# A two-layer hybrid decoder step: new order of the set-up's loads, one weight block across the seam, and VectorE's first expert work re-ordered

## The chip, the core and the metric

One Trainium2 chip, one of its cores. The metric is the device time of one launch, in microseconds (us). Engines: TensorE (PE), VectorE (DVE), ScalarE (ACT), GpSimd (POOL), and SyncE (SP), which issues most of the loads. The median of three runs of the kernel before is 2207.54 us (2205.04 to 2212.47).

## What is computed

One inference step of a decoder of two layers, for 256 prompt tokens and 8 samples of one token each, all in float32, width 1024. Each layer is

```python
def trunk_layer(x, pos, h0, conv_prev, past_lat, past_kr, p):
    h = rmsnorm(x, norm_mix)
    proj = h @ w_in            # gates, z, xBC, dt, c_q, c_kv, k_rope
    ya, h_new, conv_new = ssd_branch(...)          # Mamba-2 scan
    yb, lat_new, kr_new = mla_branch(...)          # latent attention, paged cache for the samples
    x = x + (ga * ya + gb * yb) @ w_out
    x = x + peer(rmsnorm(x, norm_ffn), peer_wq, peer_keys, peer_u, peer_v)
    return x, h_new, conv_new, lat_new, kr_new
```

`peer` is a product-key lookup: per token and head (8 heads) the two halves of a query are scored against 128 keys each, the best 16 of each half are paired, the best 16 pairs give 16 experts; each expert is one row u and one row v of 1024 numbers. Its weight is softmax of the scores times gelu(u . h), and it adds weight times v.

## The kernel before

**Set-up.** A block of its own (L477 to L530) loads the constants, the prompt rows `x`, the row of gains `nrow`, the page table, the samples' rows, and two blocks of the first layer's projection weights into the two slots of `wring`: the first 272 columns of the tail (`TAIL[0]`, with dt) and the first 256 columns of xBC. ScalarE takes the squares of both prompt tiles and a root, VectorE scales them to `h`, TensorE turns them into `ht`. All engines meet at a barrier at its end.

**The layer loop.** `Fori(0, layers)` runs one body twice. Each engine has its own program in the body; they meet in semaphores, and at the end of the body in a barrier (L535 for the end of the block, L2382 for the clearing of semaphores) before the jump back. PSUM banks are handed out by two rings of four: `wide` (banks 0 to 3, emptied by ScalarE) and `aux` (banks 4 to 7, emptied by VectorE). The order on a ring is fixed: VectorE has to empty the `aux` banks in the order in which TensorE fills them.

**Weights.** `next_block` and `load_block` (L542, L2184) use the two slots of `wring` in turn; SyncE waits until a block has been begun (`blocks_begun`) before it loads the next but one. Blocks 0 and 1 of a layer are already there at its start: the set-up has loaded them for layer 0, and the last steps of a layer (L2287 to L2292) load them for the next from `w_first`, an array in which the host lays both side by side. These last steps wait for the last gathered slot and then for both blocks. At a layer's start SyncE issues nine small loads (`vrows`, `hd`, `kvn`, `qn`); TensorE turns `vrows` after the first tail's products, before `dense(0)`, the first use of block 1.

**The expert stage.** 17 units: 8 heads for each of the two prompt tiles (16 slots a unit), and one for the samples (8 slots), 264 slots in all. For each slot GpSimd gathers 128 rows of 8 KB (u and v, 1.05 MB) by the indices of `best_experts` into a ring of 8 places (L2363). VectorE takes the products of rows and tokens (`inputs`, L1770), ScalarE the gelu (L2121), VectorE a scaled diagonal (`diagonal`, L1779), TensorE multiplies it with v and sums in PSUM (`outputs`, L1213), which occupies the `aux` banks; so the first `outputs` waits until `aux` is empty (`marks["x", 1]`). The gather of slot n waits for `outputs(n - 8)`; those of slots 3, 4, 6 and 7 wait in addition for the last readers of the weights that lie in their places: the samples' heads, `out_samples(0)`, `out(2, 1)` and `out(3, 1)`.

`best_experts(u)` is the search of unit u, a generator of 17 steps; VectorE interleaves it with the slots of the unit before, three steps a slot. Into slots 0 to 7 it also puts the late tiles (`late_tiles`): the output projection of tile 1 and of the samples is added to `x` (`out(1, 1)`, two copies of the samples' partial sums to `hp[2]`, `out(2, 1)`, `out(3, 1)`, the samples' additions at L1818), then comes the norm of these tiles (`px_mean`, `px_rows`). TensorE produces them in the same order. ScalarE's squares and root for them stand in its own `late_tiles` (L2133 and L2137).

## Time and profile before

| | us |
|---|---|
| median of three runs | 2207.54 |
| profiled run | 2213.21 |
| its span, first to last instruction | 2211.7 |
| TensorE busy | 1722.7 (78%) |
| VectorE busy | 1443.7 (65%) |
| GpSimd busy | 656.9 (30%) |
| ScalarE busy | 481.4 (22%) |
| DMA | 743.76 MB, 336 GB/s over the span |

Times in the rows are us from the span's start unless marked ns. PE is TensorE's matmuls, PEld its weight loads; a name with a final q (SPq, DVEq) is an engine's queue of instructions, where waits, branches and issues stand. `x2` counts instructions. The bracket at a row's end is the idle time before it and who ended it. PEclk is TensorE's granted clock as a share of 2.4 GHz. The first expert stage lies from 413 to 1102, the second from 1505 to 2195.

### The profile page before, as it was taken

The numbers are of one execution on the slowest core, as the hardware profiler recorded it, in microseconds if no ns is written. First come the engines' busy times: TensorE is split into PE (matmuls) and PEld (weight loads), VectorE is DVE, ScalarE is ACT, GpSimd is POOL, SyncE is SP. The second block draws the span as 40 slices with busy tenths as digits, with TensorE's granted clock in tenths as the row PEclk, the third lists the DMA queues.
The fourth block names the chain that finished last, engine by engine and source line by source line (L and its number), as shares of the span: only waits on it lengthen the run. The fifth ranks groups of instructions, "written<-read, shape, count | busy, mean of one in ns | idle before, by whom it ended". The sixth has DMA issues, their size and how long they took to land. (4 is left out here: it accounts for less than half of the span.)

```text
span 2211.7 us, 30597 instructions
## 1 busy us (share of the span) xinstructions
PE 1722.7 (78%) x11154; PEld 883.6 (40%) x11154; DVE 1443.7 (65%) x3609; ACT 481.4 (22%) x1415; POOL 656.9 (30%) x598
## 2 busy tenths in 40 slices
PE   6999989787787666666779998887878876666665
PEld 5887666532233111111168876664323321111111
DVE  3454443677787887877726554437677788787785
ACT  2235211122112121111213442112211211211112
POOL 0000000145444444454300000003444444444442
PEclk9999999977788676666799999998877886757667
DMA  5448499699999999999854385977999999999997
GB/s 195 145 138 277 140 345 320 247 393 415 419 421 421 420 396 421 421 414 418 360 163 159 117 281 194 363 271 308 390 422 415 410 422 413 416 421 421 417 417 305
DMA packets 190002, 743.76 MB, mean 336 GB/s; under 512 B 16339, under 2 KB 78220, under 8 KB 119682
## 3 DMA queue, kind: packets, MB, share of 16 engines
q0 software_dynamic: 83296, 582.18, 64.3%
q1 hardware_dynamic: 106546, 159.52, 21.1%
q8 instruction: 90, 1.47, 0.3%
q14 instruction: 70, 0.57, 0.1%
HBM read 730.38 MB, written 11.46 MB: 335 GB/s over the span
## 5 line engine op out<-in xcount | busy, mean ns | idle before, releaser
L1213 PE MATMUL ps<-arena 64*64 64x512 f32 x4096 | 755.9, 838 | 395.9 <-DVE arena L1779 375.6
L2363 POOL DMA_INDIRECT arena<-in_peer_uv,arena x528 | 617.9, 1170 | 807.1 <-PE ps L1213 663.6
L1770 DVE CUSTOM_DVE_ANT_0 arena<-arena,h 128x1024 f32<-128x1024 f32 x512 | 627.2, 1225 | 255.8 <-DMA arena<-in_peer_uv,arena 246.7
L1213 PEld LDWEIGHTS ps<-arena 64*64 64x64 f32 x4096 | 141.1, 166 | 953.0 <-DVE arena L1779 876.2
L553 PE MATMUL ps<-ht_tok,wring 128*128 128x264 f32 (+1 forms) x1536 | 368.7, 396 | 7.6 <-DMA wring<-in_w_in 7.6
L553 PEld LDWEIGHTS ps<-ht_tok,wring 128*128 128x128 f32 x1536 | 292.0, 194 | 80.7 <-issue 19.2
L2121 ACT ACTIVATE arena<-arena 128x1 f32<-128x1 f32 x528 | 105.3, 203 | 992.7 <-DVE arena L1770 978.8
L1779 DVE TENSOR_SCALAR arena<-consts,arena 128x64 f32<-128x64 f32 (+1 forms) x528 | 165.0, 313 | 26.7 <-ACT arena L2121 24.2
L553 PE MATMUL ps<-arena,wring 128*128 128x264 f32 x256 | 60.0, 388 | 0.0
L553 PE MATMUL ps<-arena,gate 128*128 128x256 f32 x256 | 58.4, 381 | 0.0
L2342 POOL DMA_DIRECT2D nrow<-in_norm_ffn x2 | 1.1, 533 | 188.6 <-PE ps L562 188.6
L1433 DVE SCALAR_TENSOR_TENSOR h<-h,exs,arena 128x1024 f32<-128x1024 f32 x16 | 20.6, 1284 | 51.0 <-ACT arena L1979 51.0
L2328 POOL DMA_DIRECT2D out<-h x16 | 8.5, 534 | 150.8 <-DVE h L1433 150.8
L553 PE MATMUL ps<-wring,ht_tok 128*128 128x272 f32 (+2 forms) x192 | 44.0, 386 | 11.9 <-ACTq L1870 11.9
L2121 ACT ACT_TABLE_LOAD x40 | 51.3, 1283 | 0.7
L553 PEld LDWEIGHTS ps<-arena,gate 128*128 128x128 f32 x256 | 47.3, 189 | 8.0 <-issue 1.6
L553 PEld LDWEIGHTS ps<-arena,wring 128*128 128x128 f32 x256 | 47.4, 190 | 7.6
L562 PE MATMUL ps<-consts,h 128*128 128x128 f32 (+1 forms) x174 | 36.8, 314 | 14.6 <-ACT h L2044 13.2
L1011 PE MATMUL ps<-arena 128*32 128x256 f32 x512 | 36.1, 401 | 12.4 <-DVEq L1584 12.4
L1701 DVE MAX8 arena<-arena 128x8 f32<-128x128 f32 x136 | 32.9, 283 | 16.9 <-ACT arena L2098 15.8
L2114 ACT ACT_TABLE_LOAD x34 | 43.6, 1283 | 0.8
L1770 DVE DVE_READ_ACCUMULATOR2_ANT arena<- 128x1 f32 x528 | 43.4, 82 | 0.0
(352 smaller groups left out, 1811.7 us busy)
## 6 DMA issues: line engine op xcount, KB each, us to landing
arena<-in_pages SPq DMA_DIRECT2D x256, 272.0 KB, 5.1
wring<-in_w_in SPq DMA_DIRECT2D x36, 1024.0 KB, 5.7
arena<-in_peer_uv,arena POOLq DMA_INDIRECT x528
h<-in_state_ssm POOLq DMA_DIRECT2D x16, 512.0 KB, 5.8
out<-h POOLq DMA_DIRECT2D x16, 512.0 KB, 4.3
wring<-in_w_ssm_proj SPq DMA_DIRECT2D x8, 1024.0 KB, 8.3
arena<-in_w_out SPq DMA_DIRECT2D x8, 1024.0 KB, 8.3
wring<-in_peer_wq SPq DMA_DIRECT2D x8, 1024.0 KB, 7.8
```

Of the source, the lines that this page charges most:

```text
L553: last = pe.matmul(dst, w(c), rhs(c), start=start and c == 0, stop=stop and c == chunks - 1)
L562: return pe.transpose(dst, src, ident[0:rows, 0:rows])
L1011: last = pe.matmul(ps[32 * g:32 * g + 32, b, 0:KV_LORA], pts[:, i % 2, j, g, :], held[:, slot, 2 * g + j, 2 * P + ROPE:KV_ROW], start=j == ...
L1213: last = pe.matmul(ps[to:to + 64, SUM_BANK[t] + i, :], diag[rows, n % DIAGS, 0:64], ring[rows, HOME[n % RING], cols], start=n in TILE_FIRS ...
L1433: dve.scalar_tensor_tensor(out=new, in0=new, scalar=exs[:, SAMPLES + s:SAMPLES + s + 1], in1=stx[:, s % 2, :, :], op0=ALU.mult, op1=ALU.ad ...
L1701: last = dve.max(top[0:r, at[half]], halves[half])
L1770: dve.tensor_tensor_reduce(ring[:, HOME[k], 0:D_MODEL], ring[:, HOME[k], 0:D_MODEL], tokens, 1.0, 0.0, ALU.mult, ALU.add, dots[:, column(n ...
L1779: dve.tensor_scalar(diag[:, n % DIAGS, 0:outs], table[:, 0:outs], gel[:, column(n)], wexp[:, column(n)], ALU.mult, ALU.mult).then_inc(sem( ...
L2114: act.activation(w, w, ACT.Exp, accum_out=wsum[:, u % 2:u % 2 + 1]).then_inc(sem("experts_exp"), 1)
L2121: act.activation(gel[:, at:at + 1], dots[:, at:at + 1], ACT.Gelu).then_inc(sem("gelu_ready"), 1)
L2328: pool.dma_start(h1[b], places[b % PLACES]).then_inc(sem(f"state_store{b % PLACES}"), 16)
L2363: pool.indirect_dma_start(ring[:, HOME[k], :], None, table, bass.IndirectOffsetOnAxis(ap=idx[:, TOPK * u + j:TOPK * u + j + 1], axis=0)).t ...
```

## The change

1. Set-up: the prompt rows load first, then the gain row, the constants, the tail's block, the page table and the samples' rows; every reader waits for what it reads. ScalarE begins with a root of a zero that VectorE writes.
2. Only the tail's block is loaded ahead, in the set-up and at a layer's end; the first xBC block is loaded at the head of the layer by SyncE, before the small loads, and TensorE waits for it at `dense(0)`.
3. The start of the expert stage: ten steps of the search of unit 1 stand before `out(1, 1)` and before slot 0; the two copies follow; slots 0 to 3 have no search steps; the late additions and the norm come one slot or more sooner, and `out(3, 1)` comes after the samples' additions, on TensorE and on VectorE.

```diff
-                sp.dma_start(consts[:, :], a["consts"]).then_inc(sem("first_loads"), 16)
-                sp.dma_start(x[:, 0:2, :], ...).then_inc(sem("first_loads"), 16)
-                sp.dma_start(nrow[:, :], ...).then_inc(sem("first_loads"), 16)
+                sp.dma_start(x[:, 0:2, :], ...).then_inc(sem("x_load"), 16)
+                sp.dma_start(nrow[:, :], ...).then_inc(sem("row_load"), 16)
+                sp.dma_start(consts[:, :], a["consts"]).then_inc(sem("consts_load"), 16)
+                sp.dma_start(wblock(0, DC, TAIL[0][1]), ...).then_inc(sem("first_loads"), 16)
                 sp.dma_start(numbers_held[0:1, :], ...).then_inc(sem("first_loads"), 16)
                 sp.wait_ge(sem("x_zeroed"), 1)
                 sp.dma_start(x[0:SAMPLES, 2, :], ...).then_inc(sem("first_loads"), 16)
-                sp.dma_start(wblock(0, DC, TAIL[0][1]), first[:, :, 0:TAIL[0][1]]).then_inc(sem("first_blocks"), 16)
-                sp.dma_start(wblock(1, DC, BLOCK), first[:, :, TAIL[0][1]:]).then_inc(sem("first_blocks"), 16)
-                sp.wait_ge(sem("first_loads"), 16 * 5)
-                sp.wait_ge(sem("first_blocks"), 32)
+                sp.wait_ge(sem("first_loads"), 16 * 3)
...
             def _(pe):
+                pe.wait_ge(sem("consts_load"), 16)
...
-                act.wait_ge(sem("first_loads"), 16 * 5)
+                act.wait_ge(sem("root_ready"), 1)
+                act.activation(rt[:, 2:3], ss[:, 2:3], ACT.Sqrt)
+                act.wait_ge(sem("x_load"), 16)
...
+                dve.memset(ss[:, 2:3], 0.0).then_inc(sem("root_ready"), 1)
...
-                dve.wait_ge(sem("first_loads"), 16 * 5)
+                dve.wait_ge(sem("row_load"), 16)
...
-                        if n >= 2:
-                            pe.wait_ge(sem(f"block{n % 2}_loads"), 16 * (n // 2))
+                        if n >= 1:
+                            pe.wait_ge(sem(f"block{n % 2}_loads"), 16 * ((n + 1) // 2))
...
                     out(2, 1)
-                    out(3, 1)
                     pe.wait_ge(sem("aux_free"), 4 + marks["sums"])
                     for half in range(2):
                         b = aux.fill()
                         aux.filled(pe.matmul(ps[0:SAMPLES, b, :], cst("sel8"), ...))
+                    out(3, 1)
...
                     ahead = best_experts(1)
+                    for _ in range(10):
+                        next(ahead)
+                    out(1, 1)
+                    for half in range(2):
+                        copy4(hp[2][:, half * 512:(half + 1) * 512])
                     def late_tiles(n):
-                        if n == 0:
-                            out(1, 1)
-                        elif n == 1:
-                            for half in range(2):
-                                copy4(hp[2][:, half * 512:(half + 1) * 512])
+                        if n == 1:
+                            out(2, 1)
                         elif n == 2:
-                            out(2, 1)
-                        elif n == 3:
-                            out(3, 1)
-                        elif n == 4:
                             for half in range(2):
...
+                        elif n == 3:
+                            out(3, 1)
+                        elif n == 5:
+                            px_mean(1, slice(46, 48))
                         elif n == 6:
-                            px_mean(1, slice(46, 48))
-                        elif n == 7:
                             px_rows((1, 2))
...
-                        for _ in range(3 if u != SAMPLE_UNIT else 6):
+                        for _ in range(0 if n < 4 else 3):
...
                     def late_tiles(n):
-                        if n == 5:
+                        if n == 4:
                             act.wait_ge(sem("aux_free"), 4 + marks["x", 1])
-                        elif n == 6:
+                        elif n == 5:
                             root(st[:, 49:51], st[:, 46:48], "px1")
...
-                    count = [2]
+                    count = [1]
                     def load_block(src, chunks, cols):
                         n = count[0]
-                        sp.wait_ge(sem("blocks_begun"), n)
+                        if n >= 2:
+                            sp.wait_ge(sem("blocks_begun"), n)
...
+                    block_of(w_in, XBC, 0)
                     vr = ssd("vrows")
...
-                    sp.dma_start(wblock(0, DC, TAIL[0][1]), first[:, :, 0:TAIL[0][1]]).then_inc(sem("first_blocks"), 16)
-                    sp.dma_start(wblock(1, DC, BLOCK), first[:, :, TAIL[0][1]:]).then_inc(sem("first_blocks"), 16)
-                    sp.wait_ge(sem("first_blocks"), 32)
+                    sp.dma_start(wblock(0, DC, TAIL[0][1]), ...).then_inc(sem("first_block"), 16)
+                    sp.wait_ge(sem("first_block"), 16)
```

The host lays `w_first` out with the tail's columns alone.

## Rows read from the trace of the kernel before

**Rows 1.** The page: DMA busy in 40 slices of 55.3 us.
```profile
DMA  5448499699999999999854385977999999999997
```

**Rows 2.** DMA, GB/s in 40 slices of 1 us from 412 to 452.
```profile
GB/s 0 0 0 205 410 418 279 377 319 385 418 410 442 401 442 426 434 418 434 410 426 410 442 393 90 16 0 0 0 98 147 393 451 401 360 385 451 401 410 426
```

**Rows 3.** Windows: length, PE, PEld, DVE, ACT, POOL busy; PEclk, DMA share, GB/s.
```profile
449.00:462.00 13.00, 13.00 (x56) 4.34 (x48) 7.08 (x14) 4.63 (x10) 6.16 (x5) 0.50 1.01 423
462.00:478.00 16.00, 12.95 (x80) 7.93 (x80) 8.31 (x27) 2.27 (x10) 5.24 (x5) 1.00 1.01 420
490.00:495.00 5.00, 5.00 (x40) 2.05 (x38) 4.67 (x12) 0.92 (x5) 1.93 (x2) 1.00 0.55 215
418.98:448.18 29.20, 18.17 (x108) 9.21 (x105) 27.38 (x74) 6.67 (x16) 11.31 (x10) 0.82 0.81 323
```

**Rows 4.** Timeline of set-up: start, us, engine, instruction, idle before it.
```profile
10.10 1.06 ACT L506 ACTIVATE h<-x 128x1024 f32<-128x1024 f32 x1 [7.82 <-DMA x<-in_x_sample]
...
12.31 1.28 ACT L509 ACT_TABLE_LOAD   x1
...
15.38 3.40 PE L499 MATMUL ps<-consts,h 128*128 128x128 f32 x16 [15.38 <-DVE h L524]
...
20.62 1.28 ACT L1882 ACT_TABLE_LOAD   x1 [6.81 <-PEq L532]
```

**Rows 5.** DMA, GB/s in 40 slices of 0.5 us from 0 to 20.
```profile
GB/s 0 0 0 0 179 298 358 406 302 345 360 401 401 401 377 311 270 287 316 361 355 359 359 357 351 349 350 346 350 346 162 6 0 0 0 0 0 0 0 0
```

**Rows 6.** L477, the first barrier: duration ns, first and last start.
```profile
L477 SPq COMPARE_BRANCH  x1: 33/33/33, 16.2 to 16.2; - x1
...
L477 DVEq COMPARE_BRANCH  x1: 47/47/47, 19.6 to 19.6; - x1
```

**Rows 7.** Issue of L2290's load, then landing of L2290's and L2291's.
```profile
L2290 SPq DMA_DIRECT2D wring<-in_w_first x2: 576/580/583, 1102.2 to 2194.6; - x2
...
DMA to landing us min/median/max: 5.8/5.9/5.9
...
DMA to landing us min/median/max: 8.0/8.1/8.1
```

**Rows 8.** L535, the seam's barrier in both layers: duration ns, starts.
```profile
L535 DVEq COMPARE_BRANCH  x2: 52/52/52, 1107.4 to 2199.8; - x2
...
L535 SPq COMPARE_BRANCH  x2: 33/36/38, 1111.1 to 2203.5; - x2
```

**Rows 9.** Timeline of TensorE at the second layer's start.
```profile
1116.53 6.06 PE L553 MATMUL ps<-wring,ht_tok 128*128 128x272 f32 x16 [10.02 <-ACTq L1870]
...
1129.54 1.15 PE L562 MATMUL ps<-consts,arena 84*128 84x84 f32 x13
```

**Rows 10.** Timeline at the start of the first expert stage.
```profile
403.85 0.49 DVE L1701 MAX8 arena<-arena 128x8 f32<-128x128 f32 x2 [5.40 <-ACT arena L2098]
...
409.51 0.09 DVE L1722 MATCH_VALUE_LOAD arena<-arena 128x8 f32 x1
...
412.72 0.37 ACT L2098 COPY arena<-ps 128x256 f32<-128x256 f32 x1 [3.65 <-PE ps L1097]
...
418.98 1.23 DVE L1770 CUSTOM_DVE_ANT_0 arena<-arena,h 128x1024 f32<-128x1024 f32 x1 [5.22 <-DMA arena<-in_peer_uv,arena]
...
420.01 7.21 PE L553 MATMUL ps<-arena,gate 128*128 128x256 f32 x32
...
427.35 1.88 PE L1159 MATMUL ps<-h,consts 128*8 128x512 f32 x4
...
437.90 8.05 PE L1213 MATMUL ps<-arena 64*64 64x512 f32 x56 [8.67 <-DVE x L1818]
...
440.19 0.97 POOL L2363 DMA_INDIRECT arena<-in_peer_uv,arena  x1 [10.96 <-PE ps L1213]
```

**Rows 11.** Timeline of GpSimd: gather 27 of layer 0, gather 8 of layer 1.
```profile
492.76 1.49 POOL L2363 DMA_INDIRECT arena<-in_peer_uv,arena  x1 [5.46 <-PE ps L1213]
...
1531.83 0.97 POOL L2363 DMA_INDIRECT arena<-in_peer_uv,arena  x1 [10.95 <-PE ps L1213]
```

More of the change, by code:

```diff
@@ L2285, in _ @@
                         count[0] += 1
-                    first = of_layer("next_first", layer).rearrange("(p c) n -> p c n", c=DC)
                     sp.wait_ge(sem("wide_full"), marks["q", 7])
                     sp.wait_ge(sem(f"slot{(SLOTS - 1) % RING}_loads"), 16 * (SLOTS // RING))
-                    sp.dma_start(wblock(0, DC, TAIL[0][1]), first[:, :, 0:TAIL[0][1]]).then_inc(sem("first_blocks"), 16)
-                    sp.dma_start(wblock(1, DC, BLOCK), first[:, :, TAIL[0][1]:]).then_inc(sem("first_blocks"), 16)
-                    sp.wait_ge(sem("first_blocks"), 32)
+                    sp.dma_start(wblock(0, DC, TAIL[0][1]), of_layer("next_first", layer).rearrange("(p c) n -> p c n", c=DC)).then_inc(sem("first_block"), 16)
+                    sp.wait_ge(sem("first_block"), 16)
                 @block.gpsimd
@@ L2433 @@
     laid["peer_uv"] = np.concatenate([np.asarray(inputs["peer_u"]), np.asarray(inputs["peer_v"])], axis=2).reshape(DEPTH * N_EXPERTS, ROW)
-    first = laid["w_in"][:, :, [*range(C_DT, C_DT + TAIL[0][1]), *range(XBC, XBC + BLOCK)]]
+    first = laid["w_in"][:, :, C_DT:C_DT + TAIL[0][1]]
     laid["w_first"] = np.concatenate([first, first[0:1]], axis=0)
```

6 lines of the change are left out of this document (3 added, 3 removed).

## The prediction, written before any run of the changed kernel

> **What bounds the kernel now.** I read the page's DMA slices first. They stand at nine tenths in two long stretches [rows 1]: these are the two expert stages, one a layer, in which GpSimd gathers 264 slots of rows of 1.05 MB each. There no compute engine sets the pace; a slot takes 1.05 MB / 0.42 MB per us = 2.5 us of transfer, and the stage lasts as long as its transfers and the times in which they run dry. So the second view is the slices of one us behind the first gather. They are full from 416, then nearly empty from 436 to 443 [rows 2]: set against 422 GB/s, these eight slices miss 6.2 us of transfer. A smaller drought lies at 490 to 495 (DMA share 0.55) [rows 3]. Outside the expert stages, in the set-up and at the two seams between layers, one chain of engines ends each barrier; there I read who comes last.
>
> **Part 1, the set-up.** ScalarE starts on the rows at 10.10, when all five loads are in, and from there to TensorE's first transpose at 15.38 runs one chain [rows 4]. The slices of 0.5 us give the bytes: they add up to 1.05 MB (the input rows alone) at 5.35 and to 2.34 MB (rows, gain row, constants) at 9.0 [rows 5]. The five loads are 2.37 MB, in by about 9.1, and the wait ended near 10.05: up to 0.9 from last byte to release. With the rows first, ScalarE starts at 5.35 + 0.9 = 6.25. Its chain to the transpose was 15.38 - 10.10 = 5.28 us, a table load of 1.28 in it (12.31); the new Sqrt ahead of the wait takes that load before the rows are there. That the squares then need no table of their own is seen in the loop, where the same order (Sqrt on a constant, squares, Sqrt) has the load at 20.62 and no other [rows 4]. So h is ready at 6.25 + 5.28 - 1.28 = 10.25. The constants are in at 9.0 + 0.9 = 9.9, the gain row before them: hidden by 0.35 us, and one for one beyond that. The first transpose moves by 15.38 - 10.25 = 5.1 us. Last to the barrier is VectorE at 19.6, SyncE comes at 16.2 [rows 6]; VectorE's goes to 14.5. SyncE now waits for 3.49 MB, by the same slices in at 12.4 + 0.9 = 13.3, 1.2 before VectorE. Bounds: 4.0 if the rows' transfer is shared with those behind it, 5.4 if a release takes 0.6. I take 5.1.
>
> Here the Trainium skill and a row differ. The row has the table load of 1.28 us, and the chain of 5.28 has room for no more. The Trainium skill (ScalarE: Activation LUTs, What ACT_TABLE_LOAD costs) counts about 2.66 us for a switch of tables, a drain included. By the page the set-up would give 1.4 us more; the trace does not bear that out here.
>
> **Part 2, the seams.** At a layer's end SyncE issues two blocks, the first at 1102.2; they land after 5.8 to 5.9 and 8.0 to 8.1 us, at 1108.1 and, issued 0.8 later, at 1111.1 [rows 7]. The second does not hold back the first (they land 3.0 us apart, which is 1.05 MB at 350 GB/s), so alone it lands at 1108.1 too. Last to the barrier is SyncE at 1111.1; VectorE comes at 1107.4 [rows 8]. Without the second block SyncE comes at 1108.1 and is still last. Gain 3.0; 3.7 at most, where VectorE is next. The end of the second layer shows the same times 1092.4 later [rows 8], so 6.0 in all.
>
> **Part 3, the block at the head of the layer.** The XBC block's load goes to the front of SyncE's queue, ahead of nine small loads: one more issue (0.5 us) and 1.05 MB before them, 5.9 us to land by the seam's block [rows 7]. TensorE reads the first small ones (the rows for vt) at 1129.54, 13 us after the layer's first product at 1116.53, and waited for none [rows 9]; behind the block they land 6 to 7 us after it. The block itself is needed 1.1 us after them. Cost nothing, under the first tail's products, with 6 us to spare; with that cover gone up to 3 us a layer. The later blocks wait for the same starts as before.
>
> **Part 4, the start of the expert stage.** Why does the transfer run dry? The ring holds eight slots, and slot 8's gather waits for slot 0's output products. TensorE starts these at 437.90, after 8.67 us of waiting for VectorE's sample additions (L1818) [rows 10]. VectorE did the late additions one a slot, between row products and search steps; before that it idled 5.22 us, from 413.76 until slot 0 landed at 418.98 [rows 10].
>
> The new order on VectorE in layer 0: at 413.76 it is through with out(0,1), and ScalarE has put out the scores of unit 1 at 412.72 + 0.37 = 413.1. Ten search steps took 403.85 to 409.51 = 5.66 for unit 0 [rows 10], so to 419.4. The other steps are taken from start to start in the same timeline. out(1,1) is 0.34 and the two copies are 1.2: 421.0. Slot 0 and its weights (1.15 + 0.46): 422.6. Slot 1, diagonal 0, out(2,1) (1.15 + 0.26 + 0.34): 424.35; TensorE has out(2,1) at 420.01 + 3.6 = 423.7. Slot 2 lands at 424.7 (three slots are in at 423.8 [rows 2], + 0.9): 0.35 of waiting; with diagonal 1 and the sample sums (1.2) 427.3. TensorE has the sums' products at 423.7 + 1.88 = 425.6 [rows 10], in time. out(3,1) now follows them and ends at 429.2; VectorE, through with slot 3 and diagonal 2 at 428.7, waits 0.5 and has it at 429.65. TensorE starts slot 0's output products at 429.8 instead of 437.90. From that start to gather 8 were 2.3 us (440.19) and to its first bytes 1.6 (98 GB/s in the slice of 441): 429.8 + 3.9 = 433.7, ahead of the ring's end at 436.3. The first drought goes whole, with 2.6 us in hand. Slot 7's gather, behind out(3,1), is issued at 429.4, with bytes from 431.6 (2 us), and is needed at 433.8: covered by 2 us.
>
> That is not yet the gain. From slot 7 on, products follow VectorE's diagonals, and the second drought (gather 27, issued at 492.76 after 5.46 us of waiting for TensorE [rows 11]) sits at the end of a chain without a transfer: TensorE full from 449 to 462 (13.00 of 13) at clock 0.50 [rows 3], then queries, scores, the search of unit 2. What moves is that chain's start, the end of slot 7's diagonal at 448.18. From 418.98 to there VectorE has 29.20 us, one wait of 1.04 in them (for slot 0's products); the row's busy 27.38 leaves 0.8 of steps between instructions [rows 3]. So 28.16 of work, the same in the new order; begun at 413.76 it ends at 441.9, and with the new waits (0.35, 0.5, and some 0.15 for the late tiles' root) at 442.9. The chain starts 5.3 us earlier, I take 5.2. The transfers would be 6.2 to 6.5 earlier, so the second drought grows by about 1.2, and the stage is 5.2 shorter. Behind it the transfers are full, and all later steps are counted by slot. In layer 1 gather 8 waits 10.95 us for TensorE in the same way [rows 11]: 5.2 again. The last unit's three steps instead of six change nothing, no search is left there.
>
> **The sum.** 5.1 + 6.0 + 0 + 2 x 5.2 = 21.5 us. The span of 2211.7 goes to 2190.2, the profiled run's 2213.21 to 2191.7. The median of the runs is 5.67 below that run: 2207.54 - 21.5 = 2186.0.
>
> **Rivals.** A, the clock stays up. TensorE's stretch from 449 to 462 ran at 1.2 GHz though it was busy throughout [rows 3]. At 2.4 GHz the transfers would set its pace, which are 6.2 to 6.5 ahead, and 3 us of the second drought could go too: 6.5 to 9.5 a layer, 24 to 30 in all, 2183 to 2177. For it: the pause of 8.67 us goes. Against: from 433 to 443 TensorE will have little to do, and the row shows a busy engine held at 0.50. 0.2. The Trainium skill (TensorE: Matmul & The Clock Gate, Part 1) has the gate follow how busy the array was of late, and by it the busy engine of that row should have been fast; the row says otherwise.
> B, the expert stage gives nothing: the second drought takes all back because ScalarE, whose other steps keep their order, holds the queries' place, or the first one stays because the output products still wait. Then 11.1 in all, 2196.4. Against it: TensorE, not ScalarE, is full in that chain. 0.17.
> C, slower. Between 462 and 478 TensorE worked 12.95 us at 2.4 GHz [rows 3]. Should the new phase hold these products and queries at 1.2 GHz, the second drought grows by 13 a layer: 26 - 21.5 = 4.5 slower, 2212. It decides from 10.8 us a layer on. 0.03.
> D, the change does less than it says: the small loads bind, or the rows land no earlier. 2 to 5 us less, 2188 to 2191. 0.05.
> The forecast has 0.55, with a range of its own from 2182 to 2190 (the bounds above and 2 us of scatter).
>
> **Range and chances.** From the far half of A, 2178, to just short of B, 2195: the forecast, D, most of A and a third of B, about 0.8. A measurement of this kernel tells 0.3% (6.6 us) from no change. Below 2200.9 lie the forecast, A, D and nearly all of B: 0.91; within 0.3% 0.06; slower 0.03.
>
> **What would show it.** ScalarE's first square near 6.2 and no table load before its root; the first barrier's last arrival near 14.5; SyncE at the seam's barrier 5.9 us after its one issue; no wait of TensorE over 1 us for L1818; gather 8 about 16.6 us after the first bytes (now 24.7) and no empty slices behind slot 7; gather 27 about 72 us after the first bytes (now 77.3), with a drought some 1.2 us longer than now. The prediction is wrong if gather 8 comes later than 19 us, gather 27 before 70 or after 75, or if TensorE waits for a small load at a layer's head.

## The result, and the profile after

The changed kernel takes 2185.98 us (median of four runs, 2180.19 to 2188.55), the kernel before 2210.01 in the same comparison (2205.04 to 2212.84): a ratio of 0.9889, interval 0.987 to 0.9908, or 24.0 us by the medians. The forecast was 2186.0 and a gain of 21.5 us. The run whose profile follows is the fastest of its four (2180.19 us, span 2178.6). The profiled run of before is slower than its median, so these two traces lie 33.0 us apart, and 9 us of that is not the change. Where this comes from is a large part of what the experiments had to settle.

Set-up, after: ScalarE's first square and the root, TensorE's first transpose, then the last arrivals at the first barrier.

```profile
6.16 1.06 ACT L505 ACTIVATE h<-x 128x1024 f32<-128x1024 f32 x1 [3.66 <-DMA x<-in_x_prompt]
...
8.58 0.20 ACT L508 ACTIVATE st<-st 128x2 f32<-128x2 f32 x1 [0.23 <-DVE st L518]
...
10.45 3.65 PE L496 MATMUL ps<-consts,h 128*128 128x128 f32 x16 [10.45 <-DVE h L524]
```

```profile
L477 SPq COMPARE_BRANCH  x1: 33/33/33, 12.5 to 12.5; - x1
...
L477 DVEq COMPARE_BRANCH  x1: 47/47/47, 14.9 to 14.9; - x1
```

Set against [rows 4, 6]: the first square 3.94 us sooner, no table load in front of the root, the first transpose 4.93 us sooner, VectorE last to the barrier at 14.9 instead of 19.6. The layer's first product starts at 15.96 instead of 20.65: 4.7 us.

The seams, after: the one load's issue and landing, and who comes last to the barrier (both layers).

```profile
L2291 SPq DMA_DIRECT2D wring<-in_w_first x2: 333/333/333, 1081.9 to 2165.4; - x2
...
DMA to landing us min/median/max: 5.0/5.0/5.0
```

```profile
L535 SPq COMPARE_BRANCH  x2: 33/36/38, 1086.9 to 2170.5; - x2
L535 DVEq COMPARE_BRANCH  x2: 52/52/52, 1087.0 to 2170.2; - x2
```

Against [rows 7, 8]: the load alone lands after 5.0 us, not after 5.8 to 5.9, so SyncE comes 3.9 us sooner after its issue. VectorE, which came 3.7 us ahead of it before, is now level with it.

The head of the second layer, after: TensorE's turn for vt, the products on the block that is now loaded at the head (1106.95), and the first products on the block behind it.

```profile
1105.88 1.14 PE L562 MATMUL ps<-consts,arena 84*128 84x84 f32 x13
1106.95 7.39 PE L553 MATMUL ps<-ht_tok,wring 128*128 128x264 f32 x32
1114.72 10.50 PE L553 MATMUL ps<-ht_tok,wring 128*128 128x264 f32 x46 [0.38 <-DMA wring<-in_w_in]
```

No wait for a small load and none for the moved block: the head costs nothing. The 0.38 us at 1114.72 are for the third block, which is loaded as before; TensorE waited 1.35 us for it in the same place of the trace before.

The start of the expert stage in layer 0, after. First the DMA engines' GB/s in 40 slices of 1 us from 400 to 440 (the first gather is issued at 401.0), then TensorE and GpSimd in the timeline.

```profile
GB/s 0 0 98 188 418 385 328 393 295 418 401 401 410 451 442 401 434 410 434 401 434 451 418 401 434 426 442 401 393 467 418 418 401 426 434 434 410 393 434 442
```

```profile
417.65 2.81 PE L1213 MATMUL ps<-arena 64*64 64x512 f32 x24 [0.58 <-DVE x L1660]
...
434.58 1.70 PE L562 MATMUL ps<-consts,h 128*128 128x128 f32 x6
...
442.66 3.83 PE L553 MATMUL ps<-ht_tok,wring 128*128 128x264 f32 x16
```

```profile
419.05 0.94 POOL L2363 DMA_INDIRECT arena<-in_peer_uv,arena  x1 [0.76 <-PE ps L1213]
...
473.01 1.49 POOL L2363 DMA_INDIRECT arena<-in_peer_uv,arena  x1 [5.29 <-PE ps L1213]
```

The eight poor slices of [rows 2] are gone. TensorE starts slot 0's output products 16.6 us after the first gather (before: 24.6) and waits 0.58 us instead of 8.67 [rows 10]; gather 8 follows after 0.76 us. Gather 27 is issued 72.0 us after the first gather (before: 79.5).

### The profile page after: what moved, and what is told of

Read it like the earlier page. It is cut to its first block and busy times, and to the rows that moved or that the text cites. A ratio compares the mean times of both kernels' runs of the same rounds, so it can differ in the third digit from the quotient of the medians.

```text
span 2178.6 us, 30595 instructions
## 1 busy us (share of the span) xinstructions
PE 1705.1 (78%) x11154; PEld 879.4 (40%) x11154; DVE 1443.5 (66%) x3610; ACT 480.5 (22%) x1415; POOL 658.2 (30%) x598
## 5 line engine op out<-in xcount | busy, mean ns | idle before, releaser
L1213 PE MATMUL ps<-arena 64*64 64x512 f32 x4096 | 744.2, 825 | 391.9 <-DVE arena L1779 383.8
L1011 PE MATMUL ps<-arena 128*32 128x256 f32 x512 | 35.2, 394 | 12.3 <-DVEq L1584 12.3
```

The lines of the kernel that those rows point to most:

```text
L1011: last = pe.matmul(ps[32 * g:32 * g + 32, b, 0:KV_LORA], pts[:, i % 2, j, g, :], held[:, slot, 2 * g + j, 2 * P + ROPE:KV_ROW], start=j == ...
L1213: last = pe.matmul(ps[to:to + 64, SUM_BANK[t] + i, :], diag[rows, n % DIAGS, 0:64], ring[rows, HOME[n % RING], cols], start=n in TILE_FIRS ...
```

## The experiments

Times in the tables are medians. The three groups of runs have each their own runs of the kernel before: 2209.3, 2210.45 and 2209.7 us.

### The parts, each by itself, and a second trace of after

**The set-up alone** (both blocks still loaded):

```
-sp.dma_start(consts ...)  -sp.dma_start(x ...)  -sp.dma_start(nrow ...)     # all "first_loads"
+sp.dma_start(x ...)       # x_load
+sp.dma_start(nrow ...)    # row_load
+sp.dma_start(consts ...)  # consts_load
 sp.dma_start(wblock(0, ...), first[:, :, 0:TAIL[0][1]]).then_inc(sem("first_blocks"), 16)
 sp.dma_start(wblock(1, ...), first[:, :, TAIL[0][1]:]).then_inc(sem("first_blocks"), 16)
+act.activation(rt[:, 2:3], ss[:, 2:3], ACT.Sqrt)     # ahead of ScalarE's first wait
```

> The kernel before with the set-up's part alone: the rows load first, each load has its own semaphore, Sqrt on a constant ahead of ScalarE's first wait; both weight blocks are still loaded there and at the seams. By the sum of places read in the two traces (the theory): ScalarE's first square near 6.2 us, TensorE's first transpose near 10.4 (before 15.38). But SyncE then waits for the second block too, 1.05 MB behind the rest: by the slices of the set-up (350 to 400 GB/s) about 3 us after the 13.3 us that I gave SyncE with one block, so the barrier ends near 16 instead of 14.5. 3.2 to 4.7 us faster than before. The rival, that the set-up's gain is given back later in the layer (a wait on the weight blocks takes it), gives 0 to 1 us in total and a shift of the later instructions that shrinks back to zero within the first 100 us.

**One block alone:**

```
-sp.dma_start(wblock(1, DC, BLOCK), first[:, :, TAIL[0][1]:]).then_inc(sem("first_blocks"), 16)   # set-up and seams
+block_of(w_in, XBC, 0)                                                                         # head of the layer
```

> The kernel before with one weight block at the start and across each seam, the next block's load at the head of the layer; nothing else. The traces of before and after give 3.5 and 3.8 us for the two seams, so 7.3 us, and 0 at the heads. The set-up gains nothing, since VectorE and not SyncE ended its barrier: 7.3 us faster, 6.0 by the prediction's term. The rival, that the head gives the seam's gain back (small loads behind 1.05 MB, TensorE waits for the rows of vt or for the block), gives 0 to 3 us in all, and would show as a TensorE wait of 1 us or more within 15 us of the layer's first product.

**The expert stage alone** (the four hunks on TensorE's sums, VectorE's late tiles and search, ScalarE's late tiles):

```
-                    out(3, 1)          # TensorE, ahead of the sample sums' products; now behind them
+                    for _ in range(10):
+                        next(ahead)
+                    out(1, 1)          # and the copies; then out(2,1), sums, out(3,1) with slots 1, 2, 3
```

> The kernel before with the expert stage's part alone (ten search steps ahead, late additions sooner, their root one slot sooner, the sample sums' products ahead of out(3,1)). Theory one (the order and the clock): TensorE starts slot 0's output products some 8 us sooner against the first gather, the chain behind slot 7 starts 3 to 3.6 us sooner, and its transposes and outputs, at 2.4 instead of 1.2 GHz, are 4 us shorter: 7.9 us in layer 0 and 7.9 to 9.8 in layer 1, 16 to 18 in all. Theory two (the prediction's term, the order alone): 5.2 a layer, 10.4 in all, with the stretch of transposes still at 1.2 GHz. Were it under 2 us, the traces' difference in the stage would belong to the two runs and not to the change.

**The changed kernel again:**

> The changed kernel once more, for a second trace. The two traces at hand differ by 33.0 us, the medians by 24.0; 7 us of the 33 arise between 195 and 385 us of layer 0 and 5 us are lost again between 1160 and 1480 in layer 1, where nothing was changed. Theory: these come and go with TensorE's granted clock in single executions (the trace of before has four short falls to 1.2 GHz in layer 0's middle and one in layer 1's, that of after none and four). Then this trace has its falls at other counts, its middle stages differ from the first trace of after by up to 7 us, and set-up (first barrier at 15.9), seams and expert stage repeat within 0.5 us. The rival, that the change itself moves the middle (other loads meet there), gives the same middle in both traces of after.

| run | median us | ratio to before | interval |
|---|---|---|---|
| set-up alone | 2207.16 | 0.9988 | 0.9977 to 0.9999 |
| one block alone | 2199.59 | 0.9964 | 0.9951 to 0.9977 |
| expert stage alone | 2198.21 | 0.9954 | 0.9937 to 0.9972 |
| after again | 2183.87 | 0.9883 | 0.9869 to 0.9898 |

The parts give 2.7, 8.0 and 10.2 us by their ratios, 20.8 together; the whole gives 25.8 here (22.5 to 28.9 by its interval). One block alone is where both traces had put it (7.3 us). The expert stage alone gives 10.2 us (6.2 to 13.9), near the forecast's 10.4 and not the 16 to 18 that I had read from the first pair of traces.

The set-up alone falls short of the 4.7 us that it gives in after (2.7 us, 0.2 to 5.1), and its trace says where. TensorE's first products of the layer, and the first on the third block:

```profile
L477 SPq COMPARE_BRANCH  x1: 33/33/33, 16.3 to 16.3; - x1
```

```profile
31.46 7.39 PE L556 MATMUL ps<-ht_tok,wring 128*128 128x264 f32 x32
40.68 1.60 PE L556 MATMUL ps<-ht_tok,wring 128*128 128x264 f32 x6 [1.83 <-DMA wring<-in_w_in]
```

SyncE, with the second block to wait for, is now last to the barrier at 16.3 (VectorE: 14.7), so the layer starts 3.3 us sooner and not 4.7: that much of the set-up's part needs the one block. TensorE then waits 1.83 us for the third block, where in the trace before it waited 0.31 us (at 41.96), and 1.3 us of the gain are left at that point. This second wait is not shown to be an effect of the set-up: in layer 0 it varies from 0 to 2.1 us over the 14 traces of this study, and it is 1.84 us in the trace of the late additions alone (below), whose set-up is that of before. What the 5 us are by which the parts fall short of the whole stays open in the same measure: 1.4 us are the barrier's, the rest is within the intervals of the four runs.

The second trace of after is the run that changed the reading. I had expected its expert stages to repeat within 0.5 us; they are 3.6 and 5.8 us longer. Each layer's expert stage, from its first to its last gather, in all the traces that matter (worked out from the gathers' issues), with TensorE's stretch behind slot 7 (from the first transpose of the later rows to the first queries, so the same six groups of instructions):

| trace | stage, layer 0 / 1 (us) | stretch (us) | slot 7's diagonal ready, after the first gather |
|---|---|---|---|
| before | 673.4 / 674.0 | 12.3 / 13.1 | +34.9 / +34.7 |
| after, first trace | 665.4 / 663.7 | 8.1 / 8.0 | +31.2 / +30.2 |
| after again | 669.0 / 669.5 | 12.3 / 12.4 | +30.0 / +29.9 |
| expert stage alone | 670.4 / 669.9 | 12.4 / 12.4 | +30.8 / +29.9 |

The same kernel, the same order, and 8.0 or 12.3 us for the same work. Windows of after (first line) and of after again, over that stretch; the columns are those of [rows 3]:

```profile
434.58:442.66 8.08, 8.08 (x52) 3.85 (x49) 4.98 (x11) 2.95 (x7) 3.38 (x4) 0.95 1.01 420
```

```profile
434.00:446.40 12.40, 12.40 (x53) 4.41 (x49) 5.23 (x12) 4.71 (x11) 5.16 (x4) 0.51 1.01 420
```

TensorE is full in both. It runs at 2.4 GHz in one and at 1.2 GHz in the other. The stretch differs by 4.3 us, gather 27 by 3.2 and 5.3 us (+75.2 and +75.3 in after again, +72.0 and +70.0 in after), the stage by 3.6 and 5.8. That the difference goes through to the stage's end can be read from the gathers: from gather 27 to the last one it is 593.1 to 595.1 us in both layers of all twelve traces in which the queries keep their place (594.0 in before, 593.4 in after, 593.8 in after again, layer 0). So the change and the clock act on the stage ahead of gather 27 alone.

The forecast's reading of before's stretch (full, clock 0.50 [rows 3]) and rival A's doubt are both right, one execution each. The Trainium skill (TensorE: Matmul & The Clock Gate, Part 1) has the gate follow how busy the array was of late. By that rule both stretches would be fast: the first trace of after agrees (0.95), the second does not, it is another row in which the array is busy throughout and held at 0.51.

What the second drought did is seen in slices of 5 us, after again first from 470 us, then after from 470, then before from 485; against 422 GB/s they miss 4.9, 2.5 and 3.7 us of transfer:

```profile
470.00:475.00 5.00, 5.00 (x19) 4.04 (x16) 4.86 (x12) 0.20 (x1) 1.02 (x1) 0.65 0.92 324
475.00:480.00 5.00, 5.00 (x39) 2.08 (x38) 4.67 (x10) 0.98 (x5) 2.55 (x2) 1.00 0.46 143
480.00:485.00 5.00, 5.00 (x34) 2.94 (x36) 3.21 (x9) 0.63 (x4) 2.91 (x3) 1.00 0.97 388
```

```profile
470.00:475.00 5.00, 5.00 (x40) 2.22 (x38) 4.85 (x12) 0.84 (x4) 1.69 (x2) 1.00 0.77 320
475.00:480.00 5.00, 5.00 (x32) 3.44 (x32) 3.11 (x9) 0.78 (x4) 3.00 (x3) 1.00 0.96 324
480.00:485.00 5.00, 4.66 (x44) 1.72 (x36) 2.92 (x6) 3.47 (x7) 4.12 (x3) 1.00 1.01 413
```

```profile
485.00:490.00 5.00, 5.00 (x19) 3.27 (x12) 4.86 (x13) 0.20 (x1) 1.02 (x1) 0.56 1.01 421
...
495.00:500.00 5.00, 5.00 (x32) 3.43 (x32) 3.21 (x8) 0.63 (x4) 2.75 (x3) 1.00 0.94 336
500.00:505.00 5.00, 4.57 (x40) 1.78 (x32) 2.71 (x7) 3.75 (x7) 4.27 (x4) 1.00 1.01 405
```

(The slice from 490 to 495 of before stands in [rows 3].) With the stretch at 1.2 GHz the second drought grows by 1.2 us, which is the forecast's figure; at 2.4 GHz it shrinks by 1.2 (layer 0 of one trace each).

**The middle of the layers.** The first pair of traces also drifts apart by 7.6 us in layer 0 between the layer's first product and its first gather, nearly all of it between 195 and 385 us, where nothing was changed, and back by 4.4 us in layer 1. Windows of before and of after, from 26 us to the first gather:

```profile
26.00:413.31 387.31, 364.58 (x2951) 288.04 (x2950) 177.43 (x372) 107.60 (x315) 17.61 (x30) 0.98 0.65 224
```

```profile
26.00:401.04 375.04, 351.76 (x2926) 279.25 (x2926) 177.15 (x371) 107.39 (x314) 15.04 (x27) 1.00 0.67 230
```

The mean clock is 0.98 in one and 1.00 in the other. Over the traces of this study (14 with the two first ones) the time from layer 0's first product to its first gather is 385.2 us + 0.52 us for each us that TensorE spent at 1.2 GHz between 26 us and that gather (correlation 0.92). Counted from the first product itself it is 0.46 (0.88), and in layer 1 0.41 (0.95). Six of the 14:

| trace | us at 1.2 GHz | first product to first gather |
|---|---|---|
| before | 17.1 | 392.7 |
| expert stage alone | 13.7 | 391.4 |
| one block alone | 6.8 | 388.7 |
| after again | 3.4 | 385.8 |
| after | 0.0 | 385.1 |
| search alone (below) | 0.0 | 384.3 |

Kernels with and without the change lie about the same line, most within 1.5 us of it; the farthest off is the trace of the late additions alone, 3.2 us above. So up to 9 us in one trace's middle go with the clock of the execution and not with the kernel; a pair of traces can't be subtracted there. The runs without a trace say the same in the large: of the twelve of the late additions alone, the fastest (2192.71 us) has a mean granted clock of 0.836 and the slowest (2217.43) one of 0.821, with a correlation of -0.93 over the twelve; of the twelve of the expert stage alone it is -0.78.

### Filling TensorE's pauses

If the clock decides about 4.3 us a layer, work for work's sake in the pauses ahead of the stretch should win them. The idle products write a PSUM bank that nothing reads:

```
+def keep_busy(n):
+    for _ in range({0: 28}.get(n, 0)):      # after: {2: 5, 3: 8, 4: 7}, and {16: 10, 17: 7, 18: 3}; second try on before: {0: 14, 7: 4}
+        pe.matmul(ps[:, wide.fill(), 0:256], ident, consts[:, 0:256], start=True, stop=True)
 for n in range(SLOTS):
+    keep_busy(n)
     outputs(n)
```

> The kernel before with 28 products of 128x256 whose result nobody reads, in TensorE's pause of 8.67 us ahead of slot 0's output products; all else as it was. The clock theory: the granted clock no longer falls 18 us behind the first gather, the transposes and outputs behind slot 7 (12.3 us at 1.2 GHz in the trace of before, 8.1 us at 2.4 GHz in the first trace of after) run at 2.4 GHz, gather 27 comes at +75.5 instead of +79.5 us behind the first gather, and a layer's expert stage is 3.5 to 4.5 us shorter though the first drought (gather 8 at +26.9) stays: 7 to 9 us in all, ratio near 0.9965. The rival, that only the order of the work on VectorE sets the second drought: gather 27 stays within 0.7 us of +79.5, the time within 1.5 us of before; if the filling holds real products back, up to 2 us slower a layer.

> The changed kernel with idle products of 128x256 (5, 8 and 7) ahead of the output products of slots 2, 3 and 4, where TensorE waits 1.5, 2.5 and 2.1 us for diagonals. The two traces of after differ in one thing there: in the first the clock is low from 24 to 34 us behind the first gather, in the second from 24 to 45 us, through the transposes; the stage is 665.4 and 663.7 us in the first, 669.0 and 669.5 in the second. The clock theory: with the pauses filled the clock stays at 2.4 GHz, gather 27 comes at +70 to +72 instead of +75.2, and the stage is 664 to 665 us in both layers, every time: 8 to 10 us faster than the typical run of after (2184), near 2175, and with less scatter. The rival (the long stages of the second trace have another cause, or the fall of the clock doesn't hang on these pauses): within 2 us of 2184, or slower by the filling, 1 to 3 us.

> The same with idle products also ahead of slots 16, 17 and 18 (10, 7 and 3), where TensorE waits 3.1, 2.1 and 0.9 us. There both traces of after have 10.2 us of low clock, in which two slots' outputs take 1.98 instead of 1.09 us and the first queries behind them 5.36 instead of 3.83: 3.3 us, ahead of a drought of about 3 us of transfer in which gather 27 waits 5.3 us for TensorE. The clock theory: these 3.3 us come off the drought, gather 27 at +68 to +69, 2.5 to 3 us a layer beyond the variant with the first filling alone, near 2169 to 2170. The rival: the drought is set by VectorE's diagonals of slots 16 to 18, and the second filling brings under 1 us in all.

> The first filling of before was twice too long: 28 products were 56 instructions and took 12.35 us in a pause of 8.67, and ahead of slot 7 a pause of 3.1 us stayed, behind which the clock fell again (38 to 52 us behind the first gather). Here 14 products (28 instructions, 6.2 us) stand ahead of slot 0's outputs and 4 (1.8 us) ahead of slot 7's, where before pauses 2.3 us. The clock theory: no low clock from 35 to 49 us behind the first gather, the stretch from slot 7's transposes to the first queries takes 8.0 instead of 12.3 us, gather 27 comes at +75.3 instead of +79.5, and a stage takes 669.3 instead of 673.7 us: 8.5 us faster in all, ratio near 0.996. The rival (the stretch is long for another reason than its clock, or its length doesn't carry through to the stage): 673 to 674 us a stage and the time within 1.5 us of before.

| run | median us | ratio | interval | stages | stretch |
|---|---|---|---|---|---|
| before, filled with 28 | 2216.22 | 1.0022 | 1.001 to 1.0034 | 675.6 / 676.0 | 12.7 / 11.9 |
| before, filled to size | 2204.9 | 0.9982 | 0.9965 to 0.9998 | 673.0 / 673.0 | 12.7 / 11.4 |
| after, filled ahead of 2 to 4 | 2180.84 | 0.9874 | 0.9857 to 0.9892 | 665.8 / 666.2 | 8.0 / 8.0 |
| after, filled in both places | 2184.31 | 0.9882 | 0.9866 to 0.9897 | 666.0 / 664.8 | 8.8 / 8.0 |

The first filling of before missed its size: one product of 128x256 is two instructions, and

```profile
427.31 12.35 PE L1202 MATMUL ps<-consts 128*128 128x256 f32 x56
```

overfills a pause of 8.67 us, so it showed only that 3.4 us on the output products cost 2 us a stage. The stretch stayed at 1.2 GHz, and the run came out 4.9 us slower by its ratio, where I had expected 7 to 9 us faster.

The filling sized to the pauses is the useful one. In layer 0 it did not hold the clock (10.2 of the stretch's 12.7 us at 1.2 GHz). In layer 1 it kept the clock up until the stretch's last outputs (2.1 of its 11.4 us at 1.2 GHz), and the stretch still took 11.4 us and the stage 673.0, against 674.0. The median is 4.0 us below before (0.4 to 7.7), between the 8.5 us of the clock theory and the 1.5 us of its rival; the two stages of its trace give 1.5 us of that, and where the rest comes from is not shown. TensorE and VectorE in that stretch, and the window around it:

```profile
1533.07 1.09 PE L1218 MATMUL ps<-arena 64*64 64x512 f32 x8 [0.41 <-DVE arena L1785]
...
1540.54 1.98 PE L1218 MATMUL ps<-arena 64*64 64x512 f32 x8 [1.41 <-DVE arena L1785]
```

```profile
1534.05 1.23 DVE L1776 CUSTOM_DVE_ANT_0 arena<-arena,h 128x1024 f32<-128x1024 f32 x1 [1.04 <-DMA arena<-in_peer_uv,arena]
```

```profile
1532.00:1536.00 4.00, 3.59 (x21) 1.94 (x25) 2.48 (x6) 1.07 (x4) 2.40 (x2) 1.00 1.02 426
```

TensorE is at 2.4 GHz in this window and waits for diagonals, VectorE waits 1.0 us for each slot, the transfers are full: behind the first drought the rows themselves are late and set the pace, and the clock's 4.3 us are not there. How much of the drought has to go first is not shown. It need not be all: the late additions alone (below) still miss 4.2 us of transfer there, against 6.2 in before, and their stretch took 7.98 us at 2.4 GHz. In after, where it is closed, the filling ahead of slots 2 to 4 held the clock in both layers, and the stretch took 7.98 us both times. The stages are 3.3 us shorter than in after again, with gather 27 at +70.6 and +71.5. I had expected 664 to 665 us and a time near 2175; the stages are 1 us longer and the median is 2180.84. The interval overlaps that of after (0.9869 to 0.9898), so this is no proven gain over it.

The second filling brought nothing: I had expected 2169 to 2170, and gather 27 at +68 to +69; it came at +71.6 and +70.8. That is what its rival said, though not for the reason that the rival gave. No slice of it is at 1.2 GHz from the first gather to gather 27, and yet:

```profile
454.68 4.58 PE L1202 MATMUL ps<-consts 128*128 128x256 f32 x20
...
464.45 1.56 PE L1202 MATMUL ps<-consts 128*128 128x256 f32 x6
465.94 1.09 PE L1218 MATMUL ps<-arena 64*64 64x512 f32 x8
466.96 3.83 PE L553 MATMUL ps<-ht_tok,arena 128*128 128x264 f32 x16
470.72 3.69 PE L1218 MATMUL ps<-arena 64*64 64x512 f32 x32
```

The idle products ahead of slot 16 (20 instructions, 4.58 us in a pause of 3.05, again about 1.5 times what fits) hold slots 16 to 18 back: against the first filling alone, slot 18's outputs end 1.9 us later behind the first gather, and the queries behind them, at 2.4 GHz, still 1 us later. What a filling of the right size would give there is not shown.

### The place of the queries

> The changed kernel with head 3's three steps on TensorE (queries, queries, scores) three, two and one slots later (behind slots 21, 24 and 27 instead of 18, 22 and 26). In both traces of after gather 27 waits 5.3 us for slot 19's outputs, which stand behind the first of these queries (5.4 us at 1.2 GHz, 3.8 at 2.4), while slot 19's diagonal is ready at about +66. Theory: what is left of the second drought (2.5 us of transfer in after) is this queue place: gather 27 at +68 to +70 in a trace whose stretch ran at 2.4 GHz and +71.5 to +73 where it ran at 1.2, 2 to 2.5 us a layer, 4 to 5 in all, near 0.986. The rival: VectorE's slots 16 to 18 with three search steps each (3 us a slot against 2.5 of transfer) set the drought, or the queries' new place makes another behind slot 21: under 1 us, or slower by up to 3.

> The same with the filling ahead of slots 2, 3 and 4, which kept the clock up in the stretch behind slot 7 (7.98 us in both layers) and gave stages of 665.8 and 666.2 us. If the two add up: gather 27 at +68 to +69, stages of 663.5 us, 8 to 12 us faster than after with its stretch at 1.2 GHz, near 2175, ratio near 0.984. If the queries' place is worth nothing: 0.987 to 0.988, as the filling alone (0.9874).

```
-        at = (2, 6, 10) if hh > 2 else (11, 12, 14)
+        at = (5, 8, 11) if hh == 3 else (2, 6, 10) if hh > 2 else (11, 12, 14)
```

2189.54 us, 0.9894 (0.9871 to 0.9918), and with the filling 2185.82, 0.9875 (0.985 to 0.99). Gather 27 did come sooner, at +66.9 instead of +70.0 in layer 1, where the stretch ran at 2.4 GHz as in the first trace of after; with the filling at +67.6 in both layers. But the stage took 663.9 us (after: 663.7), and in layer 0, at 1.2 GHz, 669.9 (after again: 669.0). GpSimd waits behind slot 21 instead, at gather 30, which needs the place of slot 22:

```profile
1574.59 1.49 POOL L2363 DMA_INDIRECT arena<-in_peer_uv,arena  x1 [4.35 <-PE ps L1213]
```

The drought moves with the queries and is paid either way. The rival holds: with the queries moved, 597.0 to 598.0 us lie between gather 27 and the last gather in the four stages of these two runs, instead of 594, so gather 27 alone no longer tells the stage's length. This trace is also the best picture of the two cases, since both are in one execution: 669.9 us with a stretch of 12.05, 663.9 with one of 7.98.

### The two halves of the expert stage's part

```
 late_only:   out(1, 1) and the copies ahead of the slots, out(2,1), sums, out(3,1) with slots 1, 2, 3; no steps ahead
 search_only: ahead = best_experts(1)
+             for _ in range(10): next(ahead)       # 0 steps with slots 0 to 3; late additions as before
```

> The kernel before with the expert stage's order of late additions alone: out(1,1) and the copies ahead of the slots, out(2,1), the sample sums and out(3,1) with slots 1, 2 and 3, the root a slot sooner; the search keeps three steps a slot from slot 0. Two theories on where the stage's gain comes from. By counting VectorE's work: ahead of slot 0's output products now stand four slots with their 12 search steps instead of five with 15, and 1.5 us of additions and copies have moved into the idle 5.2 us, so these products start 4.5 to 5 us sooner than in before (+24.6), near +20, and gather 8 near +22; the first drought is some 4.5 us shorter. The stage then gains what reaches slot 7's diagonal: about 1.5 us moved into the idle time, 1.5 to 2 us a layer, 3 to 4 in all (0.9985). Were the first drought itself what counts, it would gain 4.5 a layer, 9 in all.

> The kernel before with the ten search steps ahead alone (none with slots 0 to 3, three a slot from then on); the late additions keep their slots, with slots 0 to 4. VectorE's count: 5.7 us of steps fill the idle 5.2 us; ahead of slot 0's output products there are 13 steps instead of 15. They start 5 to 6 us sooner than in before (+24.6), near +19; gather 8 near +20. The stretch behind slot 7 starts 3.5 to 4.5 us sooner (+32.3 to +33; +36.7 in before): nearly all that both parts give together (3.6 to 4.4), since moving late additions from slot to slot takes no work off VectorE. The stage gains that, and 4.3 us more where the clock stays up in the stretch. Rival: the two halves share the gain, the search alone gives 2 us and the early additions the rest (with them alone the stretch started at +35.6, 1 us sooner).

Late additions alone: 2205.18 us, 0.9973 (0.9953 to 0.9992). Search alone: 2204.89, 0.9978 (0.9958 to 0.9998). The intervals leave 1.8 to 10.4 us for the one (6.0 by its ratio, expected 3 to 4) and 0.4 to 9.3 for the other (4.9). The medians can't say whether the halves need each other: 6.0 and 4.9 add up to 10.8, the expert stage alone gives 10.2. The traces, one of each, say that they do. Slot 7's diagonal was ready 1.4 and 2.3 us sooner than in before, with both halves 4.8 in after again (+34.9 to +30.0 in layer 0) and 4.4 in the expert stage alone, all as means of both layers: 0.7 to 1.1 us more than the two together. I had expected 1.5 to 2 for the one, which nearly came, and 3.5 to 4.5 for the other, which did not; slot 0's output products also came later than I had worked out, at +21.4 (expected near +20) and +20.8 (near +19). VectorE's waits from the first gather to slot 7's diagonal tell why: before, search alone, late additions alone, after again.

```profile
DVE arena L1770 <- DMA arena<-in_peer_uv,arena: 5.2, 1, 5.2
DVE arena L1779 <- PE ps L1213: 1.0, 1, 1.0
```

```profile
DVE arena L1770 <- DMA arena<-in_peer_uv,arena: 2.8, 3, 1.5
DVE arena L1779 <- PE ps L1213: 1.0, 1, 1.0
```

```profile
DVE h L1248 <- PE ps L1060: 2.5, 2, 1.5
DVE x L1660 <- PE ps L553: 2.4, 1, 2.4
DVE arena L1770 <- DMA arena<-in_peer_uv,arena: 0.5, 1, 0.5
```

```profile
DVE arena L1770 <- DMA arena<-in_peer_uv,arena: 1.5, 3, 0.6
```

In sum 6.2, 3.8, 5.4 and 1.5 us idle: 2.4, 0.8 and 4.7 less than before, against 2.3, 1.4 and 4.8 by which the diagonal came sooner. Two of the three agree within 0.1 us, the late additions' within 0.6. The clock apart, what moves the diagonal is VectorE's idle time there. Steps alone leave it waiting for slots, since the work between them is too short; additions alone make it wait for TensorE, since they are asked for before they are computed. Each half fills the other's waits.

The late additions' trace has its stretch at 2.4 GHz (7.98 us in both layers) and stages of 667.7 and 667.6, 5.7 and 6.4 us shorter than in before, with gather 8 at +23.7. If 4.3 us of that are the clock's, 1.4 and 2.1 are left for the order. The search's trace has it at 1.2 GHz (12.35 us in both) and stages of 670.7 and 670.9: 2.8 and 3.1 us by the order alone.

## Why the prediction was right, and where it was not

**Set-up** (forecast 5.1 us, measured 4.7). The release of the rows came at 6.16 against 6.25, SyncE at 12.5 against 13.3, VectorE at 14.9 against 14.5. The forecast was 0.4 us high, and the term mis-sized is the table load. I took its 1.28 us off the chain whole, but from the end of the squares to the root it was 1.31 us (12.29 to 13.60) and is 0.23 (8.35 to 8.58): VectorE's step on the sums had run beside the load, so only 1.08 us go. Behind that TensorE's transposes take 3.65 instead of 3.40 us; this is not the change's doing, two other traces in which the rows still load behind the constants have 3.68. The Trainium skill's 2.66 us for a switch (ScalarE: Activation LUTs, What ACT_TABLE_LOAD costs) doesn't show here in the after trace either; the saving was smaller than the load, not larger.

**Seams** (3.0 each, measured 3.7: from the last gather of layer 0 to the next layer's first product 29.8 us in before, 26.2 and 26.1 in the two traces of after, and from layer 1's last gather to the end 32.5 against 29.4 and 28.9). The step that failed is "alone it lands at 1108.1 too": alone it lands after 5.0 instead of 5.8 us, so the second load had cost the first 0.8 us. VectorE is next at 3.7 us and sets the gain, which was the upper bound.

**Head of the layer** (0, measured 0). The waits named stay away, and TensorE never waits for the moved block. The block behind it is 0 to 0.9 us late in the two traces of after (0.3 and 1.4 in before).

**Expert stage** (5.2 a layer). With the stretch at 1.2 GHz, as the forecast had it, it is 4.5 us from before to after again (673.4 and 674.0 to 669.0 and 669.5). Over all stages of the old order (before, set-up alone, one block alone: six, 673.6 on average) and of the new one (after again, expert stage alone: four, 669.7) it is 3.9. Slot 0's output products start 16.6 and 16.1 us after the first gather, forecast 429.8 - 413.3 = 16.5. Slot 7's diagonal comes 4.8 us sooner in after again, forecast 5.2: the new waits are 1.5 us and not 1.0. The term mis-sized here is these waits. The first drought is closed whole, the second grows by 1.2 us as worked out. The page's DMA line shows the same: the eighth and the 28th slice, at the start of the two stages, have 6 and 7 tenths in [rows 1] and 8 and 8 in the line of after (in part because the first stage begins 12 us, the second 20 us sooner):

```profile
DMA  6448598899999999999854475978999999999997
```

**Rival A** (the clock stays up, 6.5 to 9.5 a layer, given 0.2) is what the first trace of after shows: 8.1 us in layer 0 and 10.3 in layer 1. Its condition, that the transfers are ahead by then, is borne out by the filling of before, where they were not and 9.3 us of the stretch at 2.4 GHz gave 1.0 us of the stage. The prediction's own sign says it too: it was to be wrong with gather 27 before 70 us behind the first bytes. These come 2.2 us behind the first gather, so gather 27 stands at 69.8 and 67.8 in the first trace of after, ahead of that bound, and at 73.0 and 73.1 in the second, inside it. Where I was wrong is in treating forecast and rival as two futures of the kernel. Both occur in the same kernel, from one execution or one layer to the next. Of the eight stages traced with the change's order and no filling (after, after again, expert stage alone, queries later) three have the clock up and five not. By that the stage's mean gain is about 4.5 + 3/8 x 4.3 = 6.1 us a layer, an estimate from eight stages.

**The sum.** 4.7 + 7.4 + 0 + 2 x 4.5 = 21.1 us with the stretch at 1.2 GHz; 24.3 with the estimate of 6.1. The medians say 24.0 (20 to 29 by the interval) and 25.4. The first pair of traces adds up as well: 4.7 (set-up) + 7.6 - 4.4 (middles) + 8.1 + 10.3 (stages) + 3.6 + 3.1 (seams) = 33.0. So the set-up and stage terms were a little high, the seams low, and a gain of the clock stood with a rival. That 2186.0 was hit to 0.02 us is luck: it was worked out from a median of 2207.54 for the kernel before, which is 2210.01 in the comparison, and from a gain of 21.5 us, which is 24.0; the two errors cancel. One of its chances is off as well: below 2200.9 it counts nearly all of rival B and says 0.91, but with all of B (0.17) the sum is 0.97.

Rivals B, C and D are out: the expert stage gives its gain, nothing that ran at 2.4 GHz fell behind the change, the rows and small loads came as worked out.

What stays open is what decides, from one execution to the next, whether the clock is up in the stretch. The last pauses ahead of it are alike in the two traces of after (2.5 us, then 2.1), and filling them held it up every time (four stages of four, and two more with the queries later, against three of eight without the filling); which of them counts was not tried. Nor was any version found that beats the changed kernel by more than the intervals.

## What to carry to other kernels

An engine's idle time ahead of a ring's first full turn is worth filling with work that is due later, if it is filled from two sides, so that what one order makes it wait for is computed meanwhile: measure the gain as the idle time that went, not as the work that moved. Before two traces are subtracted, a second trace of each is needed, or at least the granted clock in the stretches that are compared; a stretch without any change in it that drifts by microseconds is the sign. A term that rests on a low clock is a term with two values, and both belong into one forecast, with their share.

## What was not expected of the hardware

- The same instructions, behind the same pauses of 2.5 and 2.1 us, ran 8.0 or 12.3 us at TensorE's two levels, in two executions of one kernel and in two layers of one execution; busy throughout either way (granted clock 0.95 to 1.00, or 0.51).
- A low clock costs about half its length where TensorE is the pace (0.52 us for each us over 14 traces), and nothing like it where transfers are (a stretch of 11.4 us, 9.3 of them at 2.4 GHz, behind the first drought).
- A weight block's load followed at once by another landed after 5.8 us, alone after 5.0.
- A product of 128x256 in f32 is two instructions of 0.22 us each at 2.4 GHz (56 in 12.35 us), which twice made a filling half as long again as its pause.
